# Rows of h 272 columns long in place of 258

## The reference

```
hn = rms_norm(x, ln1);  proj = hn @ w_in            # first stack, 1024 x 2824
x = x + concat(y_moba, y_mlstm, y_swa) @ w_out      # 1024 x 1024
u = rms_norm(x, ln2) @ w_up;  x = x + relu(u)**2 @ w_down
h = modulate(rmsnorm(x, norm1), sh1, sc1);  proj = h @ w_in_2   # second stack, 1024 x 5632
merged = sigmoid(a_ret) * ret_d + sigmoid(a_pool) * pool_d;  x = x + g1 * (merged @ w_out_2)
gate, up = split(modulate(rmsnorm(x, norm2), sh2, sc2) @ w_ffn_in_2)
x = x + g2 * ((silu(gate) * up) @ w_ffn_out_2)
```

## Time and profile before

| what | value |
|---|---|
| time, median of 3 runs | 1438.87 us |
| the profiled execution, first to last instruction | 1437.5 us |
| PE busy | 98% |
| DVE busy | 80% |
| ACT busy | 58% |
| TensorE clock granted, mean | 0.998 of full |
| DMA, mean | 207 GB/s |

### The profile page before, as it was taken

How to read it: one execution, slowest core, us unless ns; L and a number is a source line. 1 busy time by engine, 2 the same in 40 slices (tenths; PEclk the granted TensorE clock), 3 DMA queues, 4 the chain that set the end, 5 groups by cost and what they waited for, 6 DMA issues and landing times.

```text
span 1437.5 us, 25549 instructions
## 1 busy us (share of the span) xinstructions
PE 1415.0 (98%) x10339; PEld 1317.2 (92%) x10339; DVE 1145.0 (80%) x1799; ACT 828.4 (58%) x1249; POOL 10.5 (1%) x21
## 2 busy tenths in 40 slices
PE   8999999999999999999999999999999999999997
PEld 8898888889888888889999999998999999999986
DVE  7898888888898888887778777777777787778763
ACT  6776776446776775344657555444446566554552
POOL 2000000000000000000000000000000000000000
PEclk9999999999999999999999999999999999999999
DMA  9643999986446999988744578898777545778662
GB/s 256 161 140 108 283 264 266 295 224 168 134 130 187 271 260 302 280 241 229 217 139 147 178 232 221 228 249 225 222 227 214 146 147 171 233 212 227 184 185 65
DMA packets 485364, 297.13 MB, mean 207 GB/s; under 512 B 14956, under 2 KB 455792, under 8 KB 485120
## 3 DMA queue, kind: packets, MB, share of 16 engines
q1 hardware_dynamic: 483728, 292.00, 71.7%
q10 hardware_dynamic: 816, 1.84, 0.4%
q0 software_dynamic: 704, 1.66, 0.4%
HBM read 289.43 MB, written 1.05 MB: 202 GB/s over the span
## 4 chain that ended last, share of the span: by engine, by line
PE 79%; DVE 11%; ACT 5%; issue 3%; DMA 1%; SPq 0%; DVEq 0%; ACTq 0%
PE acc L1929 15%; PE acc L1928 15%; PE acc L1930 15%; PE acc L1945 8%; PE mx L1945 6%; PE acc L1946 4%; DVE w_lo L1073 4%; PE mx L1946 3%; DVE ada_acc L1163 2%; ACT w_hi L577 2%; PE acc L1960 1%; PE acc L1961 1%; PE acc L1962 1%; DMA raw<-in_w_down 1%; PE mx L2348 1%
## 5 line engine op out<-in xcount | busy, mean ns | idle before, releaser
L1073 DVE TENSOR_TENSOR w_lo<-raw,w_hi 128x1024 fp32r<-128x1024 f32 x450 | 541.3, 1219 | 113.4 <-ACT w_hi L577 111.5
L577 ACT ACTIVATE w_hi<-raw 128x1024 fp32r<-128x1024 f32 x450 | 458.5, 1049 | 138.7 <-DMA raw<-in_w_in 83.8
L1928 PE MATMUL acc<-h,w_hi 128*128 128x258 f32 (+1 forms) x1776 | 507.7, 286 | 3.4 <-DVE h L1100 2.4
L1929 PE MATMUL acc<-h,w_hi 128*128 128x258 f32 (+1 forms) x1776 | 502.9, 283 | 0.0
L1930 PE MATMUL acc<-h,w_lo 128*128 128x258 f32 (+1 forms) x1776 | 497.4, 280 | 0.0
L1928 PEld LDWEIGHTS acc<-h,w_hi 128*128 128x128 f32 x1776 | 334.3, 188 | 10.8 <-issue 4.8
L1930 PEld LDWEIGHTS acc<-h,w_lo 128*128 128x128 f32 x1776 | 337.5, 190 | 0.0
L1929 PEld LDWEIGHTS acc<-h,w_hi 128*128 128x128 f32 x1776 | 335.1, 189 | 2.6 <-issue 2.4
L1945 PE MATMUL mx<-u,w_hi 128*128 128x512 f32 x864 | 304.1, 396 | 0.0
L1946 PE MATMUL mx<-u,w_lo 128*128 128x256 f32 x864 | 241.2, 279 | 0.0
L1945 PEld LDWEIGHTS mx<-u,w_hi 128*128 128x128 f32 x864 | 162.1, 188 | 37.4 <-DVE u L1877 0.3
(11 more groups left out here) (294 smaller groups left out, 1661.7 us busy)
## 6 DMA issues: line engine op xcount, KB each, us to landing
raw<-in_w_in SPq DMA_DIRECT2D x132, 512.0 KB, 4.2
ada<-in_w_ada SPq DMA_DIRECT2D x96, 512.0 KB, 4.9
raw<-in_w_ffn_in SPq DMA_DIRECT2D x88, 512.0 KB, 4.9
raw<-in_w_up SPq DMA_DIRECT2D x64, 512.0 KB, 5.7
raw<-in_w_down SPq DMA_DIRECT2D x64, 512.0 KB, 6.1
raw<-in_w_out SPq DMA_DIRECT2D x32, 512.0 KB, 4.1
raw<-in_w_ffn_out SPq DMA_DIRECT2D x32, 512.0 KB, 4.1
raw<-in_w_ret_o SPq DMA_DIRECT2D x16, 512.0 KB, 4.1
```

What stands on the lines that cost most here:

```text
L577: nc.scalar.activation(w_hi[:, n % NS], raw[:, n % NS], ACT.Copy).then_inc(hi_ready, 1)
L1073: V.tensor_tensor(w_lo[:, n % NS], raw[:, n % NS], w_hi[:, n % NS].bitcast(F32), ALU.subtract).then_inc(lo_ready, 1)
L1928: mm(outp, w_hi[:, i % NS, k], rhs[:, k, 0], start=k == 0, stop=False)
L1929: mm(outp, w_hi[:, i % NS, k], rhs[:, k, 1], start=False, stop=False)
```

## The change

A constant HPAD = 272 is the length of a row of `h2`, 1,088 bytes, in place of W = 258, 1,032 bytes. Readers and writers of h name the columns 0 to W or S to W explicitly, where they took the whole row before. The 14 columns behind are neither written nor read. On every engine the instructions are the same, in the same order and of the same sizes; only addresses differ. `h2` is 896 bytes longer on each partition, and what is placed behind it moves up by as much.

```diff
 W = S + 2
+HPAD = 272
...
-        h2 = sb("h2", [P, KT, 2, W], F32R)
+        h2 = sb("h2", [P, KT, 2, HPAD], F32R)
...
-                cn.link(V.tensor_copy(h_hi[:, :, S:], both))
-                V.tensor_tensor(h_lo[:, :, S:], both, h_hi[:, :, S:].bitcast(F32), ALU.subtract)
+                cn.link(V.tensor_copy(h_hi[:, :, S:W], both))
+                V.tensor_tensor(h_lo[:, :, S:W], both, h_hi[:, :, S:W].bitcast(F32), ALU.subtract)
...
-                        slab(p0 + i, h2, acc[:, i % 4, 0:W],
+                        slab(p0 + i, h2[:, :, :, 0:W], acc[:, i % 4, 0:W],
...
-                    slab(f0 + s, h2, acc[:, s % 4, 0:W],
+                    slab(f0 + s, h2[:, :, :, 0:W], acc[:, s % 4, 0:W],
```

## The result

The changed kernel took 1446.19 us in the median of four runs (1444.27 to 1448.65), the kernel before 1438.76 beside it (1438.13 to 1440.89). The ratio is 1.0057, 95% interval [1.0045, 1.0068]: some 8 us slower by the ratio, 7.4 by the medians. The forecast was 1437.3 us and no change that could be told; its range ended at 1442.5.

The account below looks back on a forecast made before the run. PE's own pace was taken as the bound (busy 98%). Terms 0 - 1.3 - 0.3 = -1.6 us gave 1435.9 on the profiled span, 1437.3 us as median; likeliest range 1434.5 to 1440.5, wider range 1431.0 to 1442.5.

Parts of the forecast that it names:

- Term 1: 258-column matmuls on h, 1,408 triples in 176 slabs: no change, 0 us taken, ends -4.8 and +1.2 us.
- term 2: MLP pairs of 512- and 256-column matmuls on h, 512 in 64 slabs: -1.3 us, ends -2.4 and +1.1.
- Term 6: Everything behind h moves by 896 bytes: 0 us taken; u's pairs bounded by -1.8 and +4.1 us.
- Terms 2 and 3: MLP pairs on h: -1.3 us; 256-column projections on h, 1,104 matmuls in 46 slabs: -0.3 us.
- Terms 4 and 5: Pool branch's weights on h, 118.3 ns a matmul, and DVE's and ACT's writers of h, 480 and 510 ns: 0 us each.
- The slower rival: Aligned rows are worse: 258-column triples +2.8 us, MLP pairs +1.1, together 1442.8 us, with u's pairs 1446.9; chance 0.15.
- The penalty rival: 258-column matmuls: 3.4 ns beside unaligned h_lo is real and alignment removes it, -4.8 us; 1431.4 us in all; chance 0.30.

## Why the prediction was wrong

**Reading the bound** was right: the change acted through PE's pace and arrived nearly in full when it was a loss. Over the runs the sum of paces and the measured ratio go together: +9.0 us and 1.0057 for the kernel after, +3.7 and 1.0028, +7.6 and 1.0044, +4.9 and 1.0029, +7.2 and 1.0047 for 896 bytes behind h, 272 with 128 behind, 274, and 272 with h 128 bytes later. Small sums and gains don't follow: with h 32 bytes later the paces give some +0.7 us and the clock 2.3 (1.0016), with 1,056 bytes behind h -2.4 and -0.1, with rows of 288 and 160 bytes behind -5.6 and -1.4 to -2.2. Of a gain in pace less than half arrived in these runs, and why isn't shown.

**Term 1 failed**, and it is most of the error. The step was: "I take 0, because the total is nearer to y's, and two separate layouts obeying columns/2.4 + 12 ns (11.9 for y, 11.7 for h) leaves no room for an alignment term." It measured +6.7 us, outside my bounds of -4.8 and +1.2. That two layouts gave nearly the same number was coincidence: y alone took 117.3, 118.7 or 120.0 ns a matmul depending on where it lay. I had the warning in the earlier trace rows, u's pairs at 346.7 and 353.5 ns on the same addresses, and used it for term 2 only. The upper bound was y's pace, one observed layout, and one layout bounds nothing about another.

**Term 6 failed** too: "Relative to 64 bytes nothing changes; I take 0." The layout with 896 bytes behind h shows that this shift costs y 1.5 and u 2.0 us, with h untouched. My bound of +4.1 for u held, y was left out.

**Terms 2 and 3** had the right sign: -0.8 for the pairs (forecast -1.3; they take a pace of 350.0 ns of their own, neither of u's two) and -0.5 for the 256-column slabs (forecast -0.3). Terms 4 and 5 were right: 118.3 ns and 481 and 510 ns.

The slower rival came closest (1442.8, with u 1446.9, at 0.15): its decision point, a slab over 2.875 us, was passed, and the price was 37.8/8 = 4.7 ns a triple instead of 2.0. That 1446.9 lies within 1 us of the measured time is luck: it had +2.8 for the wide slabs, +1.1 for the pairs and +4.1 for u, where the profile has +6.7, -0.8 and +2.1, and nothing for y's +1.5. Its reason was wrong too. Rows of 288 are more aligned and ran at 2.855, and rows of 274, unaligned as before, at 2.874. The penalty rival fell with the h_lo pass, which kept its 121.5 ns when aligned.

For 256-column passes, starts 8 bytes off against aligned starts at the same distance cost 54 ns for 24 passes, 2.2 ns a pass; in the kernel after, 11 ns for 8 h_lo passes make 1.4. The Trainium skill, "SBUF — State Buffer", section "SBUF: two separate sides", says that each cross to a new 16-byte line costs. By it such a row crosses one line more when it starts 8 bytes off, which I had priced at 1.85 ns, so these two agree with it. But with aligned starts, where the count of lines is the same, 256 columns of h took from 2805.0 ns (rows of 264) to 2839.6 (of 272) and y from 2816 to 2880. For 258 columns the rule foretells no change, and the runs differ by up to 46 ns a slab (2854.9 to 2900.4). There the measurement decides: the rule isn't the mechanism that matters, at either width.

**What stays open** is the mechanism. Shown: PE's pace on h changes with the distance between the rows it reads, with their start within 128 bytes and with their width; a shift of h by 128 bytes left it as it was. Shown too: y, and h in some layouts, can hold different paces in different stretches on the same addresses, and the same again when the kernel is run again. Not shown: which unit makes it so, and what hands a pace on from one stretch to the next. Whether y's 1.5 us in the kernel after come from y's new place or from h's new rows is open as well: moving y with h's old rows brought them, and so did h's new rows with y back in its place relative to 1,024 bytes. The weights never moved, so how the rows lie to them was tried by that one shift of 128 bytes only.

## What to carry to other kernels

Where PE is the bound, moving a tensor is a change of its own: time the move alone, with padding and the old rows, since part of what you measure can belong to the neighbours, here some 40%. Padding that puts them back relative to 1,024 bytes is no cure: it gave u its old paces back and y not. Don't bound a new layout by one old one; read the nanoseconds a slab in each stretch, and try two or three row lengths, since a sweep from 258 to 304 gave -0.1 to +0.6% with no rule that foretold the order. "Aligned to 64 bytes" settles nothing: at a distance of 272 it helped the 256-column matmuls and hurt the 258-column ones, and at 288 the 258-column ones were quicker than before.

## What the hardware showed that I had not expected

- A slab's time can be the same to a nanosecond. Slabs of 258 columns took 2860.0 ns in each of 134 places and again in a second profile; other layouts gave 2800.0, 2840.0 and 2880.0 with no slab more than a nanosecond off. Others again mix a few such values, as the run truly 8 bytes off does.
- The same loop on the same addresses can hold either of two paces for a whole stretch, 2.773 or 2.828 us for u's pairs and 2.848 or 2.880 for y, and take the other in a later one.
- Of the starts tried, 32 bytes past a multiple of 64 was the best for y and u: 2.773 throughout for u, and for y 2.816 us against 2.848 or 2.880, though with rows of 258 only half of y's slabs took it.
